# Mixer scan of a two-block network: the first two heads' rows and weightings move into the token-major projection, and the states' products and sums alternate with the heads

## What is computed

```
u_f, z, xbc, dt = split(h @ w_in)           # 256 | 768 | 1792 | 24 columns
cm, xs, bm      = silu(conv3(xbc))          # 4 groups, 12 heads of 64, 128 states per head
seg    = exp(a_cs[t] - a_cs[s]), t >= s     # within chunks of 128 tokens, per head and direction
y_diag = (cm . bm) * seg @ (xs*dt)
states = bm^T (xs * dt * decay to the chunk's end)             # per chunk
h[c+1] = h[c] * decay of chunk c + states[c]                   # in sequence, h[0] from the context
y_off  = (cm . h[c]) * exp(a_cs)
y      = (y_fwd + y_bwd + d_skip*xs) * silu(z), normed by group
out    = concat(fourier(u_f), y) @ w_out
```

## Time and profile before

| | |
|---|---|
| median of three executions | 3544.07 us (3543.44 to 3544.64) |
| the profiled execution | 3546.27 us, of which the span is 3544.9 us |
| PE busy over the span | 3452.6 us, 97% |
| DVE, ACT, POOL busy | 1655.3, 1427.3, 1224.2 us |
| the stretch of the change | about 744 to 913 us of the span |

### The profile page before, as it was taken

One profiled execution on the slowest core, in us unless ns is written; L12 is line 12 of the kernel. 1 busy time (PEld: TensorE's weight loads), 2 busy tenths in 40 slices (PEclk: granted clock), 3 DMA queues, 4 the chain that ended last, 5 costly groups with the idle time before them and its releaser, 6 DMA issues.

```text
span 3544.9 us, 44797 instructions
## 1 busy us (share of the span) xinstructions
PE 3452.6 (97%) x17264; PEld 2747.0 (77%) x17264; DVE 1655.3 (47%) x3091; ACT 1427.3 (40%) x2422; POOL 1224.2 (35%) x549
## 2 busy tenths in 40 slices
PE   6999999988999999999999999999999999999998
PEld 4888899885788887877776788887877776778887
DVE  7977466666510116644542343233764453234142
ACT  3223455555432223444444343343354443334242
POOL 2555200000044443434332434444424332334443
PEclk9999999999999999999999999999999999999999
DMA  8565355221133332222222222323323222223332
GB/s 317 192 223 196 126 186 171 84 84 48 42 104 94 98 92 93 90 66 87 84 86 76 89 87 91 102 91 114 96 69 89 79 69 95 82 79 98 99 94 85
DMA packets 118564, 376.42 MB, mean 106 GB/s; under 512 B 15440, under 2 KB 16336, under 8 KB 117968
## 3 DMA queue, kind: packets, MB, share of 16 engines
q1 hardware_dynamic: 115872, 367.88, 32.2%
q10 hardware_dynamic: 2480, 5.68, 0.5%
HBM read 359.86 MB, written 2.10 MB: 102 GB/s over the span
## 4 chain that ended last, share of the span: by engine, by line
PE 89%; DVE 5%; ACT 3%; issue 1%; DMA 1%; POOL 1%; SPq 0%; ACTq 0%; DVEq 0%; POOLq 0%
PE ps L1440 27%; PE ps L1442 26%; PE ps L1441 26%; PE ps L1700 2%; PE ps L1719 2%; PE ps L1682 1%; PE ps L1483 1%; ACT b L1782 1%; PE ps L1678 1%; PE ps L1742 1%; PE ps L1753 1%; DVE b L2215 1%; PE ps L1491 1%; DMA b<-in_w 0%; DVE b L2378 0%
## 5 line engine op out<-in xcount | busy, mean ns | idle before, releaser
L2707 POOL TENSOR_TENSOR b<-b,b 128x1024 fp32r<-128x1024 f32 (+1 forms) x501 | 1155.0, 2305 | 2249.5 <-ACT b L1782 2246.6
L1440 PE MATMUL ps<-b,b 128*128 128x512 f32 (+1 forms) x4720 | 1789.9, 379 | 41.3 <-DVE b L2215 9.7
L1442 PE MATMUL ps<-b,b 128*128 128x512 f32 (+1 forms) x4720 | 1752.4, 371 | 0.0
L1441 PE MATMUL ps<-b,b 128*128 128x512 f32 (+1 forms) x4720 | 1752.2, 371 | 0.0
L1440 PEld LDWEIGHTS ps<-b,b 128*128 128x128 f32 x4720 | 889.1, 188 | 269.5 <-issue 80.5
L1442 PEld LDWEIGHTS ps<-b,b 128*128 128x128 f32 x4720 | 889.4, 188 | 160.0
L1441 PEld LDWEIGHTS ps<-b,b 128*128 128x128 f32 x4720 | 890.1, 189 | 155.5 <-issue 5.5
L1782 ACT ACTIVATE b<-b 128x1024 fp32r<-128x1024 f32 (+2 forms) x622 | 607.7, 978 | 322.4 <-PE ps L1442 310.3
L2340 DVE CUSTOM_DVE_ANT_0 b<-b,b,b 128x1024 bf16<-128x1024 f32 x112 | 225.4, 2012 | 30.4 <-DMA b<-in_ada 19.4
L1843 ACT ACTIVATE b<-b 128x512 fp32r<-128x512 f32 (+1 forms) x110 | 64.9, 590 | 369.9 <-DVE b L2259 267.2
L2250 DVE SCALAR_TENSOR_TENSOR b<-ps,b,b 128x511 f32<-128x511 f32 x88 | 66.0, 750 | 248.6 <-ACT b L1833 248.6
(11 more groups left out here) (236 smaller groups left out, 2401.5 us busy)
## 6 DMA issues: line engine op xcount, KB each, us to landing
b<-in_w SPq DMA_DIRECT2D x458, 512.0 KB, 3.5
b<-in_ada SPq DMA_DIRECT2D x88, 512.0 KB, 5.2
b<-in_w SPq DMA_DIRECT2D x80, 384.0 KB, 3.0
b<-in_w SPq DMA_DIRECT2D x80, 320.0 KB, 2.9
b<-b SPq DMA_DIRECT2D x176, 64.0 KB, 2.0
b<-in_const SPq DMA_DIRECT2D x24, 256.0 KB, 3.8
b<-in_x SPq DMA_DIRECT2D x2, 1024.0 KB, 12.0
out<-b SPq DMA_DIRECT2D x8, 256.0 KB, 2.0
```

What stands on the lines that cost most here:

```text
L1440: pe.matmul(out, a[0], b[0], start=first, stop=False)
L1441: pe.matmul(out, a[0], b[1], start=False, stop=False)
L1442: return pe.matmul(out, a[1], b[0], start=False, stop=last)
L2707: then(pool.tensor_tensor(wlo[j % NS][:, 0:nk * w], raw[j % NR][:, 0:nk * w], whi[j % NS][:, 0:nk * w].bitcast(F32), ALU.subtract), "lop", j)
```

## The change

Three things change.

1. The uf stage's background is put in at a rate of 1.6 instead of 1.3 and has 21 steps instead of 14. The two `turn` steps come first, and seven steps that stood at the head of the z stage join it: `bc(0)`, `es(0)`, `sx(0)`, `bc(1)`, `sx(1)`, `es(1)`, `ss(0)`.
2. The z stage's background starts with `hs(0)` and has 79 steps instead of 86. `ss(y+1)` and `hs(y)` are put in one by one between the steps of heads 0 to 3. From head 4 on the order of the background is the old one.
3. `h0(g, d)` uses bank 6 + d, and `bt(g)` uses bank 6 + g mod 2, instead of the next free rotating bank.

```
-    B = [do("h0", g=0, d=0), do("h0", g=0, d=1)] + last + [do("h0", g=1, d=0), do("h0", g=1, d=1)]
-    for g in range(4):
-        B += [do("bt", g=g)] + ([do("h0", g=2 + g // 2, d=g % 2)])
-    S += weave(F, B, 1.3)
+    sx, ss, hs = ([do(kind, d=y % 2, x=y // 2) for y in range(6)] for kind in ("sx", "ss", "hs"))
+    h0 = [do("h0", g=y // 2, d=y % 2) for y in range(8)]
+    bc, es, md = ([do(kind, h=h) for h in range(12)] for kind in ("bc", "es", "md"))
+    bt = [do("bt", g=g) for g in range(4)]
+    B = last + h0[:2] + [bc[0]] + h0[2:4] + [es[0], bt[0], h0[4], bt[1], h0[5], sx[0], bc[1], bt[2], h0[6], bt[3], h0[7], sx[1],
+                                             es[1], ss[0]]
+    S += weave(F, B, 1.6)
...
-    scan = sx[:2]
-    for y in range(6):
-        scan += [ss[y], hs[y]] + sx[y + 2:y + 3]
-    B = []
-    for h in range(14):
+    B = [hs[0], ss[1], md[0], sx[2], bc[2], hs[1], ss[2], es[2], sx[3], hs[2], ss[3], md[1], sx[4], bc[3], hs[3], ss[4], sx[5],
+         hs[4], ss[5], es[3], hs[5], do("eb", k=0), do("u1", k=0), bc[4], md[2]]
+    for h in range(4, 14):
...
# number(), step h0:
-            s["bank"] = brief()
+            s["bank"] = 6 + s["d"]
# number(), step bt:
-            s["bank"] = brief()
+            s["bank"] = 6 + s["g"] % 2
```

More of the change, by code:

```diff
@@ L468, in gnorm @@
         return [do(kind, hf=hf, o=o) for kind, o in steps]
-    sx, ss, hs = ([do(kind, d=y % 2, x=y // 2) for y in range(6)] for kind in ("sx", "ss", "hs"))
-    scan = sx[:2]
-    for y in range(6):
-        scan += [ss[y], hs[y]] + sx[y + 2:y + 3]
-    B = []
-    for h in range(14):
+    B = [hs[0], ss[1], md[0], sx[2], bc[2], hs[1], ss[2], es[2], sx[3], hs[2], ss[3], md[1], sx[4], bc[3], hs[3], ss[4], sx[5],
+         hs[4], ss[5], es[3], hs[5], do("eb", k=0), do("u1", k=0), bc[4], md[2]]
+    for h in range(4, 14):
         k = h // 2 - 1
-        if h == 3:
-            B, scan = B + scan, []
-        if h % 2 and k >= 0:
+        if h % 2:
             B += [do("eb", k=k), do("u1", k=k)]
[L481 to L486, removed]
+        B += es[h:h + 1] + bc[h + 1:h + 2] + md[h - 1:h]
         if h % 2 == 0 and k > 0:
```

## The result

The changed kernel takes 3554.42 us (median of 7, 3552.29 to 3556.50) against 3544.64 us for the kernel before, timed beside it (median of 7, 3539.32 to 3546.77). The ratio is 1.0029 with a 95% interval of 1.0019 to 1.0039: slower by 9.8 us at the medians. Forecast were +8.0 us and 3552.0 us.

What follows compares the result with a forecast made beforehand. PE, busy 97% of the span, was taken as the bound, so time comes from its waits and half-clock episodes. 9.9 - 5.4 + 3.5 = +8.0 us on the median gave 3552.0 us; range 3541 to 3560, own range 3551 to 3556.

Steps and rivals of the forecast that it cites:

- Gain at the front, -3.4: uf stage, before the first h0: turns first remove 1.7 us of waiting and one 1.7 us half-clock episode.
- h0(2,0), 4.35 us: uf stage: PE waits 4.35 us behind ACT's table load, exponentials and split, then DVE; with a half-clock episode, +4.9 us.
- Banks, +2.7: uf stage: bt and h0 steps sharing banks 6 and 7 wait for copies and hand-overs, +2.7 us, bounds 0.5 and 4.
- ss(1), ss(3), ss(5): 4.4, 3.1, 1.8: z stage up to u1(0): PE's waits in us at these state sums, each with a half-clock episode; u1(0) 9.9 us behind.
- After u1(0), -5.4: From u1(0) to the end of the first fo1: later background steps come seven places earlier, 35.6 us against 41.0.
- The late part, +3.5: After the first fo1: fo2 +0.8, table loads +0.5, output projection's second step waiting 5.0 us +2.4; last norm unchanged.
- rival C: Late part gains nothing because u1 and es still meet at a bank (bc(5) waits 2.5 us): 3556 us; chance 0.10.
- five signs named in advance: h0 over 3 us, table load between copies, ss over 3 us twice, no 2.5 us L2502 wait, output projection 4 to 6.
- Rival A: Chains in front of the splits don't bind; h0(2,0) waits under 1.5 us: 3536.3 us, faster; chance 0.13.
- B: Rival: half of the losses are given back, waits there but shorter, +3.3 us, 3547.4 us, no change; chance 0.38.
- part 3: The prediction's section on the kernel after u1(0), where the new order was to pay: -5.4 us, then +3.5 us later.
- The prediction's rule: Each PE wait of 1.8 us or more is followed by a half-clock episode, priced at 1.7 us.

Runs made afterwards that it cites:

- Run 2: Kernel before with only the two turns put ahead of the initial states in the uf stage: 3540.51 us, ratio 0.9986.
- Run 4: Changed kernel with the exponential's table loaded right behind the copy of turn 9: 3550.74 us, ratio 1.0022.
- run 1: Kernel before with only the other banks (h0 in 6 + d, bt in 6 + g mod 2), old order and rate: 3544.02 us, ratio 0.9998.
- Run 7: Changed kernel with an empty step ahead of yv(1), so the fifth z tile's evacuation stands in front of it on DVE: 3554.09 us, ratio 1.0025.
- Run 6: Changed kernel with es(11) and md(10) in front of eb(4) and u1(4) instead of behind them: 3551.02 us, ratio 1.0019.
- run 10: Kernel before with the two turns first, hs(4) directly behind ss(4), and es(4) ahead of md(2): 3530.33 us, ratio 0.9965.
- run 3: Changed kernel with es(0) put behind bt(0) and h0(2,0) instead of in front of them: 3557.07 us, ratio 1.0031.
- Runs 4 to 6: Changed kernel with one edit each: table loaded early, 3550.74 us; es(1) back in z behind hs(0), 3550.52; es(11) and md(10) earlier, 3551.02.

## Why the prediction was right

The direction, the size and the order of the terms held. By its own steps, with the trace after shifted by 0.76 us (uf's first matmul is at 745.29 there and at 744.53 before):

- **Gain at the front, -3.4.** The 2.6 us became 0.86. Run 2 shows 4.2 us by itself.
- **h0(2,0), 4.35 us.** Measured 4.36, by the chain as written. Run 4 takes the table load out and gets 1.4 back. The rule of the Trainium skill (ScalarE: Activation LUTs, What ACT_TABLE_LOAD costs) that another 1.38 us of drain follow would, as an estimate, have made it 5.7. The load starts 0.02 us after the copy ahead of it ends and the exponentials, at 757.05, 0.02 us after the load's end: this trace doesn't show the drain.
- **Banks, +2.7.** Too large. Only 0.75 us are seen, and run 1 finds no cost. z's first matmul stands at 775.05, 774.3 aligned, where 776 was predicted.
- **ss(1), ss(3), ss(5): 4.4, 3.1, 1.8.** Measured 3.89, 2.94, 1.72. The last had no loss at half clock; the first had two lots of 1.7 us. u1(0) starts at 812.6 aligned, predicted 814.3: 8.2 behind instead of 9.9.
- **After u1(0), -5.4. This is the step that failed.** The old 2.5 us for es(4) did go. But from u1(0) to the end of the first `fo1` 39.7 us pass and not 35.6, so the lead gave back 1.3 us. The text priced bc(7) and bc(9) and let eb(2) pass. eb(2) wants two banks when bc(7), u1(1)'s parts and z's fifth tile hold the others, and waits 3.18 us for z's product behind yv(1), with 1.7 us at half clock. Run 7 shows that it is the pair of banks, not the place.
- **The late part, +3.5.** Measured 2.9. The 5.0 us of the output projection are 1.75 + 2.72, the first of them for a bank that es(11)'s minima free, which the text didn't have. Run 6 takes es(11) from between the `fo3` steps, and 0.71 us are left there. The last norm keeps its 2.7 us, but not its time at half clock: 1.7 us that the text had wrong.

An overpriced term (banks, 1.9 too much) and a missed one (eb(2), 3.2 and its clock) partly made up for each other, which the sum alone would not show. That the forecast's range was hit owes something to luck: 3554.4 us is nearer to rival C's 3556 than to the 3552.0 forecast. And of the five signs named in advance, `ss` waiting over 3 us came once (3.89, 2.94) and not twice, and the output projection's second step waited 2.72 us, not 4 to 6; the other three came. Rival A is refuted at its own point, 4.36 us where 1.5 would have decided. B and C are not the case either, though C's idea, that the later order gains next to nothing, was the right one about part 3. Its reason was not: no bc step waits 2.5 us for `es`.

## What to carry to other kernels

Before moving a step earlier, write down what it puts in front of the next weight split on each in-order engine, not only where it finds idle time: here 3.7 us of ACT in front of a 1 us split made PE wait 4.4 us, and 1.3 us less of it made the wait 1.4 us shorter. Walk the order engine by engine with the measured durations, and give every step that takes two buffers both of its releasers. Edits of one place that put the awaited step ahead of unrelated work (two turns, one `hs`) gained 11 us; the change, with seven steps moved, a new order behind them and a higher rate, lost 10.

## What the runs showed of the hardware

The granted clock is a large part of the small differences. In this stretch it took 1.7 us (run 10) to 12.2 us (run 3). The time lost at 0.50 came in lots of 1.7 us, or of 3.4 us, in or behind a wait of PE, and single microseconds of the kernel after show it while PE is fully busy:

```profile
764.00:765.00 1.00, 1.00 (x7) 1.00 (x6) 0.00 (x0) 0.00 (x0) 0.00 (x0) 0.50 0.68 279
782.00:783.00 1.00, 1.00 (x4) 1.00 (x4) 0.96 (x3) 0.00 (x0) 0.00 (x0) 0.50 0.23 90
798.00:799.00 1.00, 1.00 (x4) 0.90 (x4) 1.00 (x2) 0.00 (x0) 0.00 (x0) 0.50 0.00 0
```

The prediction's rule, one lot behind each wait of 1.8 us or more, held in the kernel before alone. In run 10 one wait of four (2.30, 1.89, 1.78, 2.69) had it behind it, and in run 3 single waits had two lots. The stretch less its waits goes from 132.9 to 142.2 us over the twelve traces; less the time lost at half clock too, from 130.0 to 132.1. So the sum of work, waits and clock holds to about 2 us, and the 0.1 us between before and after is closer than it does in general. Runs 4 to 6, whose waits are 1.5 to 2.4 us below the changed kernel's, are 3.4 to 3.9 us faster at the median. One profile can't settle such differences: run 7's profiled execution took 3547.6 us, its median is 3554.1. Whether the lots fall by chance or follow the order of waits is left open.
